# A two-block transformer on one core: the second block's attention scores as three products of rounded and remaining parts, with its tables and last columns rearranged

## The reference, cut to what matters

```python
def swiglu(x, w_gu, w_down):                      # w_gu (1024, 2*2816)
    gate, up = jnp.split(x @ w_gu, 2, axis=-1)
    return (jax.nn.silu(gate) * up) @ w_down

y = swiglu(rmsnorm(h, ffn1_pre_g[l]), ffn1_w_gu[l], ffn1_w_down[l])
h = h + 0.5 * rmsnorm(y, ffn1_post_g[l])
u = rmsnorm(h, mix_pre_g[l])
qa, ka, va, qb, kb, vb, qc, kc, vc, gl = jnp.split(u @ w_in[l], split_at, axis=-1)
oa = neighbourhood_attention(heads(qa, 8), heads(ka, 8), heads(va, 8), na_rpb[l])
ob = sliding_window_attention(rope(qb, 8), rope(kb, 2), heads(vb, 2), sw_sink[l])
oc = differential_attention(rope(qc, 8), rope(kc, 8), vc, lam, lam_init, subln_g[l])
merged = sum over n of sigmoid(gl_n + b_gate[l, n]) * ([oa, ob, oc][n] @ w_branch[l, n])
h = h + rmsnorm(merged @ w_out[l], mix_post_g[l])
```

## Time and profile before

| | us |
|---|---|
| median of three runs | 1633.79 (1631.08 to 1634.36) |
| the profiled execution, its own time | 1631.56 |
| its span, first to last instruction | 1629.8 |
| TensorE busy | 1569.5 |
| VectorE busy | 1050.8 |
| ScalarE busy | 870.7 |
| GpSimd busy | 137.7 |
| read from HBM | 290.77 MB, 179 GB/s over the span |

### The profile page before, as it was taken

The page is one execution under the profiler, slowest core; times in us unless marked ns, Lnnn a source line. Parts: engine busy times, 40 slices in busy tenths (PEclk is TensorE's granted clock), DMA queues, the critical chain, the costliest instruction groups (busy, mean ns, idle before and its releaser), DMA issues.

```text
span 1629.8 us, 21547 instructions
## 1 busy us (share of the span) xinstructions
PE 1569.5 (96%) x7668; PEld 1292.3 (79%) x7668; DVE 1050.8 (64%) x1742; ACT 870.7 (53%) x1526; POOL 137.7 (8%) x163
## 2 busy tenths in 40 slices
PE   3989999999999999999999999999999999999998
PEld 3867787788887787877788887888778887778886
DVE  6977877666556456686765547565646568675553
ACT  2666567554445556564644446444555656454442
POOL 0520021000000300022000000000120002100000
PEclk9999999999999999999999999999999999999999
DMA  9974573365555724646555555655583454665652
GB/s 346 300 243 156 167 244 129 106 205 178 184 193 166 197 90 136 181 136 207 192 184 179 191 184 182 199 175 181 168 219 118 123 164 139 207 201 173 202 178 73
DMA packets 149191, 293.25 MB, mean 180 GB/s; under 512 B 10214, under 2 KB 23316, under 8 KB 149084
## 3 DMA queue, kind: packets, MB, share of 16 engines
q1 hardware_dynamic: 143168, 276.60, 52.6%
q0 software_dynamic: 4800, 12.29, 3.3%
q10 hardware_dynamic: 1116, 2.99, 0.5%
HBM read 290.77 MB, written 1.06 MB: 179 GB/s over the span
## 4 chain that ended last, share of the span: by engine, by line
PE 83%; DVE 6%; DMA 4%; ACT 3%; POOL 2%; issue 2%; SPq 0%; DVEq 0%; POOLq 0%; ACTq 0%
PE pb L463 78%; PE pb L467 4%; DMA raw<-in_w_in 3%; DVE wl L1457 1%; POOL st L2334 1%; DMA raw<-in_w_ada 1%; ACT wh L870 1%; DVE xt_l L1454 1%; ACT pb L870 1%; DVE mkv L1454 1%; DVE h L1454 0%; POOL cg L2365 0%; POOL bc L2350 0%; DMA bias_scratch<-mk 0%; ACT xt_h L870 0%
## 5 line engine op out<-in xcount | busy, mean ns | idle before, releaser
L870 ACT ACTIVATE wh<-raw 128x1024 fp32r<-128x1024 f32 (+1 forms) x484 | 505.9, 1051 | 435.5 <-PE pb L463 398.1
L1457 DVE TENSOR_TENSOR wl<-raw,wh 128x1024 fp32r<-128x1024 f32 (+1 forms) x484 | 582.0, 1219 | 210.0 <-ACT wh L870 206.1
L463 PE MATMUL pb<-wh,xt_h 128*128 128x512 f32 (+2 forms) x1536 | 593.7, 387 | 6.1 <-ACT xt_h L870 3.3
L463 PE MATMUL pb<-wh,xt_l 128*128 128x512 f32 (+2 forms) x1536 | 585.3, 381 | 2.6 <-DVE xt_l L1454 1.7
L463 PE MATMUL pb<-wl,xt_h 128*128 128x512 f32 (+2 forms) x1536 | 581.8, 379 | 0.0
L463 PEld LDWEIGHTS pb<-wh,xt_l 128*128 128x128 f32 x1536 | 290.2, 189 | 65.1 <-DVE xt_l L1454 10.2
L463 PEld LDWEIGHTS pb<-wh,xt_h 128*128 128x128 f32 x1536 | 290.3, 189 | 61.8 <-issue 10.1
L463 PEld LDWEIGHTS pb<-wl,xt_h 128*128 128x128 f32 x1536 | 290.3, 189 | 52.4 <-issue 2.2
L2334 POOL TENSOR_TENSOR st<-st,cols 128x1 f32<-128x1 f32 (+2 forms) x56 | 58.6, 1053 | 1084.3 <-DVE st L1454 836.6
L463 PE MATMUL pb<-wh,big_h 128*128 128x512 f32 x352 | 138.7, 394 | 0.0
L463 PE MATMUL pb<-wl,big_h 128*128 128x512 f32 x352 | 138.6, 394 | 0.0
(11 more groups left out here) (227 smaller groups left out, 1497.9 us busy)
## 6 DMA issues: line engine op xcount, KB each, us to landing
raw<-in_ffn_w_gu SPq DMA_DIRECT2D x176, 512.0 KB, 4.5
raw<-in_w_in SPq DMA_DIRECT2D x148, 512.0 KB, 4.2
raw<-in_ffn_w_down SPq DMA_DIRECT2D x88, 512.0 KB, 3.9
raw<-in_w_ada SPq DMA_DIRECT2D x48, 512.0 KB, 5.3
raw<-in_w_out SPq DMA_DIRECT2D x32, 512.0 KB, 4.0
raw<-in_w_branch SPq DMA_DIRECT2D x24, 512.0 KB, 3.5
raw<-in_w_in SPq DMA_DIRECT2D x8, 416.0 KB, 4.8
G<-in_na_rpb POOLq DMA_DIRECT2D x32, 96.0 KB, 9.4
```

The source lines that it names most:

```text
L463: return e.matmul(o, a, b, start=start, stop=stop)
L870: return e.activation(o, a, func, **kw)
L1457: return e.tensor_tensor(o, a, b, op)
```

## The change

It does six things. (1) In the second block q and k of all three attentions are stored rounded (`mqt`, `mkz` become float32r), VectorE writes the remaining parts into new tiles (`na_l`, `sw_l`, `df_l`), and the scores are q*k + q*k_low + q_low*k. The turns alternate q, k, q, k. A unit's scores wait only for the blocks that they use. (2) No tile is cleared: ScalarE writes both halves of `mkz` in full height, scaled by a column that is one on one head's rows and zero on the other's (`head_rows`); the same in the first block with the gains. (3) The column gains come with the other rows, and b_ada's last third is not loaded there. (4) `G` and `nab` lie behind all the tiles of the feed-forward, and `G` is loaded during the first one. (5) The last gate and up products of 256 columns become one of 512, each chunk with one transfer for each side. (6) `cst` is loaded later, the ones are set by GpSimd, and TensorE makes 5 and 3 products more whose result nobody reads.

```diff
-    qts = [sb(f"mqt{i}", [128, 4, 256], F, mx) for i in range(2)]
-    kz = [sb("mkz0", [128, 4, 512], F, mx), sb("mkz1", [128, 1, 512], F, mx)]
-    nab = sb("nab", [128, 48, 64], F, mx)
-    G = sb("G", [128, 48, 64], F, mx)
+    qts = [sb(f"mqt{i}", [128, 4, 256], R, mx) for i in range(2)]
+    kz = [sb("mkz0", [128, 4, 512], R, mx), sb("mkz1", [128, 1, 512], R, mx)]
...
+    low = ExitStack()
+    df_l = [sb(f"df_l{n}", [128, 4, n], R, low) for n in (256, 512)]
+    na_l = [sb(f"na_l{n}", [128, 4, n], R, low) for n in (256, 512)]
+    low.close()
+    sw_l = [sb("sw_l0", [128, 4, 256], R, low), sb("sw_l1", [128, 1, 512], R, low)]
+    low.close()
+    nab = sb("nab", [128, 48, 64], F, mx)
+    G = sb("G", [128, 48, 64], F, mx)
...
+        def turn_split(q, k):
+
+            for j in (0, 2):
+                for g in (q, k):
+                    if j < g[2]:
+                        turn_heads(g[0], g[1], g[2], 128, g[3], part="ql", only=j)
...
-                        last = mm(b.rearrange("p (j n) -> p j n", n=256)[:, :, 0:first["nk"]], first["both"]["q"],
-                                  first["both"]["k"], True, True)
+                        o, z = b.rearrange("p (j n) -> p j n", n=256)[:, :, 0:first["nk"]], first["both"]
+                        last = mm(o, z["q"], z["k"], True, z["ql"] is None)
+                        if z["ql"] is not None:
+                            mm(o, z["q"], z["kl"], False, False)
+                            last = mm(o, z["ql"], z["k"], False, True)
...
+        def keep_busy(n):
+
+            w.wait_ge(*at("x"))
+            for _ in range(n):
+                mm(banks[0][:, 0:256], ident, h[:, 0, 0:256], True, True)
...
         turn_row(0, 0)
         turn_row(0, 1)
+        keep_busy(5)
         list(rows_of_ada(0, 2))
...
+                keep_busy(3)
                 turn_row(0, 2)
                 turn_row(0, 3)
...
-            for j in range(6):
-                n = 512 if j < 5 else 256
...
+            gemm((s, "up", 5), XT, 0, key, wg, 2560, 512, "evd", two_sides=True)
+            turn_hid(4)
...
-                if zeros:
-                    w.wait_ge(*at("zeros", *zeros))
-                    ac_(upper_half(dst[:, j:j + m, :]), from_[0:64], scale=scale if scale == 1.0 else scale[0:64])
-                    ac_(lower_half(dst[:, j:j + m, :]), from_[64:128],
-                        scale=scale if scale == 1.0 else scale[64:128]).then_inc(*up("qk", s, j))
+                if sides:
+                    w.wait_ge(*at("cols"))
+                    ac_(dst[:, j:j + m, 0:256], from_, scale=sides[0])
+                    ac_(dst[:, j:j + m, 256:512], from_, scale=sides[1]).then_inc(*up("qk", s, j))
...
+        def turn_split(q, k, old=()):
+
+            for o in old:
+                w.wait_ge(*at(*o))
+            for j in (0, 2):
+                for s, nblk, hi, lo in (q, k):
+                    if j >= nblk:
+                        continue
+                    m = min(2, nblk - j)
+                    from_ = rot()[:, 0:m * 256].rearrange("p (c n) -> p c n", n=256)
+                    w.wait_ge(*at("qk", s, j))
+                    if s is q[0]:
+                        tt(lo[:, j:j + m, :], from_, hi[:, j:j + m, :].bitcast(F), ALU.subtract).then_inc(
+                            *up("ql", s, j))
+                        continue
+                    w.wait_ge(*at("cols"))
+                    for z in range(2):
+                        n = slice(256 * z, 256 * z + 256)
+                        m_ = stt(lo[:, j:j + m, n], from_, head_rows[z], hi[:, j:j + m, n].bitcast(F), ALU.mult,
+                                 ALU.subtract)
+                    m_.then_inc(*up("ql", s, j))
...
+            w.wait_ge(*at("nab", l))
+            turn_split(((s, "naq"), 4, qts[0], na_l[0]), ((s, "nak"), 4, kz[0], na_l[1]))
...
+        def bias_table(s, l):
+
+            f_ = d["na_rpb_2"][l]
+            for hh in range(8):
+                w.wait_ge(*at("evd", (s, "up" if hh % 2 else "gate", hh // 2), 1))
+                for r in range(2):
+                    dst = G[64 * r:64 * r + 64, :, :].rearrange("p (h u) w -> p h u w", u=6)
+                    e.dma_start(dst[:, hh], bass.AP(
+                        tensor=f_.tensor, offset=f_.offset + (5 - r) * 31 - 48 + 465 * hh,
+                        ap=[[1, 64], [31, 6], [1, 64]])).then_inc(*landed("G", l))
...
                     bcast(f"ffn{kind[1]}_post_g_2", l, 0, DM, (s,), ("evd", (s, "down", 512), 1))
+                    if kind == "f1":
+                        bias_table(s, l)
...
+            if len(src.shape) == 4:
+                sides = chunk_view(raw[c % NRAW], c).rearrange("p k (g f) -> p k g f", g=2)
+                for g in range(2):
+                    e.dma_start(sides[:, :, g, :], src[:, :, g, :]).then_inc(*landed(f"raw{c % NRAW}", c))
+                continue
```

More of the change, by code:

```diff
@@ L219, in groups, with both @@
     return [chunks[:head]] + [[c] for c in chunks[head:len(chunks) - tail]] + [chunks[len(chunks) - tail:]]
[L222 to L232, removed]
+def both(q, k, nk, blk, ql=None, kl=None):
+    cut = [v.rearrange("p (j n) -> p j n", n=256)[:, :, 0:nk] if v is not None else None for v in (k, kl)]
+    return {"q": q, "k": cut[0], "ql": ql, "kl": cut[1], "j": blk // 2 * 2}
 def heads(v, d):
@@ L350, in build @@
         n_rows += n
+    for name in ("moba_q_g", "moba_k_g", "mla_q_g", "mla_k_g"):
+        row_of[name] = n_rows
+        n_rows += NL
+    row_of["head_rows"] = n_rows
+    n_rows += 2
     bc_of, bc_in, n_bc = {}, [], 0
@@ L374, in stat @@
         return st[:, stat_of[name]:stat_of[name] + n]
+    head_rows = [col("head_rows", r) for r in range(2)]
     ident = cst[:, C_ID:C_ID + 128]
@@ L552, in to_xt_rows, with turn_heads @@
                 last.then_inc(*up("tr", s, t, c))
-        def turn_heads(s, src, nblk, width, ready):
-            for j in range(0, nblk, 2):
+        def turn_heads(s, src, nblk, width, ready, part="qk", only=None):
+            for j in range(0, nblk, 2) if only is None else (only,):
                 m = min(2, nblk - j)
-                b = rot("qk", s, j)
+                b = rot(part, s, j)
                 for i in range(m):
@@ L957, in to_xt_rows, with turn_split, turn_heads @@
                             scale=cscale(c + j)).then_inc(*up("xh", s, t, c + j))
-        def turn_heads(s, nblk, dst, width, old=None, scale=1.0, zeros=None):
-            for j in range(0, nblk, 2):
+        def turn_split(q, k, old=None):
+            for j in (0, 2):
+                for s, nblk, dst, sides in ((*q, None), (*k, head_rows)):
+                    if j < nblk:
+                        turn_heads(s, nblk, dst, 128, old=old, sides=sides, only=j)
+        def turn_heads(s, nblk, dst, width, old=None, scale=1.0, sides=None, only=None):
+            for j in range(0, nblk, 2) if only is None else (only,):
                 m = min(2, nblk - j)
@@ L1174, in act @@
             w.wait_ge(*at("gp"))
-            turn_heads(("mobak", l), 4, ktz, 128, scale=gp[:, 2 * l:2 * l + 1], zeros=("moba", l))
+            turn_heads(("mobak", l), 4, ktz, 128, sides=[gp[:, 3 * l + z:3 * l + z + 1] for z in range(2)])
             side.add(attention("moba", l), NU + 3)
@@ L1297, in turn_hid, with ev_last @@
                 to_xt((s, "hid", j), 4 if j < 5 else 2, BIG, 4 * j)
-            for j in range(6):
-                n = 512 if j < 5 else 256
+            def ev_last(g, t, ps):
+                v = temp(("evd", (s, "gate", 5), t))
+                w.wait_ge(*at("mm", g, t))
+                ac_(v[:, 0:256], ps[:, 0:256], ACT.Tanh, scale=keep[:, 2 + t:3 + t]).then_inc(
+                    *up("tanh", (s, "gate", 5), t))
+            for j in range(5):
                 if j == 0:
-                    gemm((s, "gate", j), XT, 8, n, ev_gate, head=STAG, between=between)
+                    gemm((s, "gate", j), XT, 8, 512, ev_gate, head=STAG, between=between)
                 else:
-                    gemm((s, "gate", j), XT, 8, n, ev_gate)
-                gemm((s, "up", j), XT, 8, n, nothing)
+                    gemm((s, "gate", j), XT, 8, 512, ev_gate)
+                gemm((s, "up", j), XT, 8, 512, nothing)
                 if j:
                     turn_hid(j - 1)
+            gemm((s, "up", 5), XT, 8, 512, ev_last)
+            turn_hid(4)
             side.add((turn_hid(5) for _ in range(1)), 1)
```

181 lines of the change are left out of this document (93 added, 88 removed).

## The result

The changed kernel runs in **1612.47 us** (median of 4 runs, 1611.37 to 1614.55) beside 1632.43 for the kernel before (median of 4 runs, 1630.35 to 1634.36, three of them those of the table above): a ratio of 0.9879, 95% interval 0.9861 to 0.9897, or 20.0 us less. The forecast was 1613.2, or 20.6 less. The profiled execution took 1614.55 us, its span is 1612.7; between the two profiled executions lie 17.1 us of span.

What follows compares the result with a forecast made beforehand. TensorE was taken as the bound, busy 1569.5 of 1629.8 us. Terms -8.6 + 2.4 - 7.2 - 2.5 - 1.7 - 3.0 = -20.6 us gave 1611.0 profiled, 1613.2 as median; its own range 1606 to 1621.

Steps and rivals of the forecast that it cites:

- Scores: Second block: three rounded products at 0.68 us replace a full-precision one at 0.86, over 48 pairs: -8.6 us.
- The fourth turn: Neighbourhood and differential head turns: the fourth waits for a PSUM bank VectorE now reads, 0.6 us x 4: +2.4 us.
- The table sooner: Both mixers: loading the bias table during the first feed-forward removes holes and a clock fall: -7.2 us.
- Rival 4: First feed-forwards, w_gu chunks of products 1 to 8: 32 table loads starve them, 24 us, total 1637; chance 0.03.
- rival 2: Head turns: VectorE becomes late, so nab and the lower parts show, 10.8 us back, total 1624; chance 0.06.
- Merge: Last gate and up: 48 products of 512 columns replace 96 of 256, 0.62 us x 4 feed-forwards: -2.5 us.
- cst later: Front: moving the 696 KB load of cst behind the modulation: -1.7 us, bounds -1.7 and 0.
- Dummies: Front: 5 and 3 dummy matmuls fall into TensorE's holes, then z waits for xt_l: 0, bounds -2 and +2.
- GpSimd and w_ukv: First block: GpSimd's relief starts k's powers sooner, and w_ukv's load may avoid the broadcasts: -3.0 us, between 0 and -6.
- the three places that the prediction names: TensorE's about 47 holes over 0.2 us: nearly all in the first 36 us, 82 to 90 us, and both mixers' starts.

Runs made afterwards that it cites:

- e1: Changed kernel with one full-precision product of the rounded q and k for the scores in place of three products: 1619.84 us.
- e9: Changed kernel with the fourth turn of the neighbourhood and differential heads in idle PSUM bank 7: 1608.72 us, on another chip, ratio 0.9837 to the kernel before.
- e2: Changed kernel with the bias table's loads issued at the mixer's start again, as before the change: 1626.53 us.
- e4: Changed kernel with NSTAT 896 again in place of 912, so later tiles start 64 bytes lower: 1615.25 us.
- e7: Kernel before the change with only NSTAT set to 912, so later tiles start 64 bytes higher: 1627.2 us.
- e3: Changed kernel with the last gate and up products as two of 256 columns again: 1614.34 us.
- e8: Changed kernel with the load of cst issued ahead of oh again: 1614.25 us.
- e6: Changed kernel without the 5 and 3 dummy products: 1613.44 us.
- e5: Changed kernel with GpSimd issuing the gain vectors' broadcasts behind the powers for k: 1612.39 us.

## Why the prediction was right, and where it was not

The forecast time and case came true, and none of the rivals is needed: the scores, the turns, the merge and cst did what was forecast, within 1.2 us each, and the table's move brought most of what it should. That the sum came within a microsecond is luck: -3.0 us for GpSimd's relief did not come, and 3.0 us that no term had came from the address of the tiles. The parts as they are found below, by stages (-8.1 + 2.9 - 6.2 - 2.3 - 1.6 - 3.0), make -18.3 us, and -19.3 with the 1.0 of the dummies, for the 20.0 of the medians.

- **Scores**, -8.6 forecast, -7.4 in the medians and -8.1 by stages (e1). Right in kind; the size is off mainly by the first of the three products, which takes 0.31 us after transposes (569.72 to 570.03) and not 0.227. The step "I take 0.227, since two of the three have a rounded product just before them" priced all three by two. The three take 0.78 and not 0.68; of the 0.10 us that this costs, 0.08 come back ahead of them, where the products start sooner after the transposes: 0.16 x 48 = 7.7.
- **The fourth turn**, +2.4 forecast, 2.86 in four holes, and 2.9 gone from the mixers when the bank is another one (e9). The chain of evacuation, copy, VectorE's 0.69 and hand-over was right (three turns of 0.44 are 1.32, not 1.35, which changes nothing).
- **The table sooner**, -7.2 forecast. It can't be had by taking it back, since e2's 14.1 us has the lower parts behind nab as well. By stages: the mixers gained 12.45 us; less 8.1 for the scores and 1.0 for the addresses (e4), and with 2.86 of holes to make good, 6.2 are left. Against the profile of e7, whose tiles start where the changed kernel's do, the same sum gives 9.15 - 8.1 + 2.86 = 3.9. The cause was right; what failed in part is "3.63 + 1.7 + 1.87 = 7.2 us less", which took the holes of one profiled execution for the table's price, where e7 shows the first at 0.53 us without a fall of the clock and with the table as late as before. So 4 to 6 us, by profiles. Rival 4 did not come, but not for the reason that I gave. A share of 0.91 for 0.60 (the same 90 us in the kernel before) is 27.9 us for 16 loads, 1.7 us each and not 0.75, and the chunks' median landing of 8.9 us is past the lead of about 8 us from which I had this rival decide. TensorE waited for none of them, and ScalarE for 1.8 us in all from 340 to 430: the lead is longer than I took it to be, by how much is open. The rule of the Trainium skill (DMA: Bandwidth & Descriptors, Why small descriptors are slow (HBM only)), by which these loads would take an estimated 6 us, is further off still.
- **VectorE late at the turns** (rival 2) is refuted by the 0.7 us holes: nab starts at 550.95 and takes 3.35 us, so it is over before the turns need VectorE. Without the table's move it would have come true in a worse form, as e2 shows. That these two parts hang together was in the text as "2 x 3.4 us would stand in front of the new lower parts", but I had not priced what comes on top of it when the weights are late too.
- **Merge**, -2.5 forecast, -2.4 in the rows, -2.3 by stages and -1.9 in the medians (e3).
- **cst later**, -1.7 forecast, 1.6 us at z in the profiles and 1.8 in the medians (e8). **Dummies**, 0 forecast within 2 each way, 1.0 (e6), less than the spread. The wait at xt_l that was to eat it did stand there (0.91 for 0.70).
- **GpSimd and w_ukv**, -3.0 forecast between 0 and -6: it gave nothing. TensorE was 1.89 us ahead of the kernel before at xt_l (43.28 for 45.17), ahead of this stretch, and 2.08 at 122.25, behind it. This is the step that failed. Its first half happened (3.9 us of holes became 1.78). Its condition, that the broadcasts no longer collide with w_ukv's load, was not met: they now go out at 66.25 to 71.62 and w_ukv is on the chain for 10.27 us. And meeting it was not enough either: with the hole taken away (e5) other waits, nearly all for ScalarE, grew in its place until at 103.59 only 0.3 us were left. From 60 to 135 us TensorE holds only 27% of the changed kernel's chain, and the loads of w_ukv and w_in 24%; I had costed single holes as if TensorE bounded there.
- **What the forecast did not have**: the 64 bytes of NSTAT, 2.8 us in the changed kernel (e4) and 5.2 in the one before (e7). The text had no price for that constant.
- **A reading that was wrong**: of TensorE's holes over 0.2 us in the kernel before, 11 of 45 lie in the three places that the prediction names (35.7 us), not nearly all. The other 34 hold 16.7 us, spread over the span, and no term went after them.

By profiled executions the first block took as long as before (-0.10 us), though z's start and e8 point to some 2 us less, and e1 to e4, with the same front, reach its end at 329.53 to 330.49, 2 to 3 us before the changed kernel's 332.49. The granted clock covers at least part of that. The changed kernel's profile has falls at 120 to 130 and at 190, which e9's, with the same work there, does not:

```profile
120.00:125.00 5.00, 3.40 (x15) 2.98 (x16) 4.13 (x14) 4.36 (x11) 1.75 (x2) 0.71 0.09 15
125.00:130.00 5.00, 5.00 (x20) 4.08 (x19) 3.87 (x8) 1.20 (x2) 1.53 (x1) 0.61 0.65 211
190.00:195.00 5.00, 5.00 (x22) 4.61 (x21) 4.40 (x8) 4.21 (x9) 0.52 (x1) 0.66 0.24 54
```

```profile
120.00:125.00 5.00, 3.82 (x22) 3.31 (x22) 4.65 (x18) 3.89 (x8) 2.81 (x2) 1.00 0.26 55
125.00:130.00 5.00, 3.30 (x29) 2.83 (x28) 4.96 (x9) 2.65 (x5) 0.46 (x1) 1.00 0.65 221
190.00:195.00 5.00, 3.81 (x21) 3.31 (x21) 4.49 (x9) 3.42 (x8) 0.00 (x0) 1.00 0.67 191
```

e9 reaches the block's end at 330.06, the changed kernel at 332.49. The median of the runs fell by 20.0 us and the span of the profiles by 17.1 because the changed kernel's profiled execution was the longest of its four (2.1 us above the median), and that of the kernel before lay 0.9 below its median. One profiled execution is not fine enough for terms of 1 or 2 us in a stage where the clock falls at places that differ from one execution to the next.

## What to carry to other kernels

Before putting new work on an engine behind an operation that can be late, make that operation early first: here the same table at its old place cost 4 to 6 us as long as the scores' operands did not stand behind it, and 14.1 once they did. Don't take the holes of one profiled execution for a price: the same hole was 3.63 us in one and 0.53 in another of nearly the same kernel. Where a second engine comes to read a PSUM bank, count when the bank is free again and give the next user an idle one (2.9 us). In a stretch where TensorE has many small holes, don't add up the holes: take one away in a run and see whether its neighbours grow.

## What the hardware did that I had not expected

- A shift of 64 bytes in where later tiles start changed the time from one matmul to the next of the down product from 0.2290 to 0.2270 us, always according to NSTAT: 57.71 to 57.72 us per 252 in the two kernels with 896, 57.17 to 57.20 in the twelve with 912. By stages that is 3.0 us in all (e4). By the tile sizes big goes from 64 bytes past a multiple of 128 to a multiple of it; other shifts were not tried, so that rule is only argued.
- The full-precision product started 0.08 us later after its transposes than a rounded one does (0.43 and 0.35), so the way in belongs to the price of an operation.
- A load of 96 KB in 256-byte pieces took 1.7 us of the DMA share beside the weights' stream. Sixteen of them over 90 us doubled the landing time of the 512 KB transfers (4.5 to 8.9 us), at no cost in TensorE's time.
- A DMA share above 1.0 does not by itself tell how long TensorE will wait: from 535 to 560 it was 1.04 with a hole of 3.63 us (before) and 1.01 with one of 0.53 (e7).
- The places where TensorE's granted clock falls from the upper of its two levels differ between executions of the same work. In means over 5 us: 0.66 at 190 us in the changed kernel, 1.00 there in e9, with TensorE busy 5.00 and 3.81 of those 5 us.
